# First block's opening on one core: the last modulation chunk in two halves, the first U products ahead of it, the U weights in pieces, the angle tables sooner

## What is computed

```python
mod = jax.nn.silu(c) @ w_ada + b_ada               # 1024 -> 3 * 1024
shift, scale, gate = jnp.split(mod, 3, axis=-1)
h = rms_norm(x, norm_g) * (1 + scale[:, None, :]) + shift[:, None, :]
proj = h @ w_in                                    # q, k, v, gates, u, z_s
...
dt = jnp.exp(log_dt)[:, None]                      # the state space mixer
lam_bar = jnp.exp(lam * dt)                        # complex: powers need sines and cosines
b_bar = ((lam_bar - 1.0) / lam)[..., None] * lax.complex(b_re, b_im)
```

## Time and profile before

| | us |
|---|---|
| three runs: lowest, median, highest | 1003.12, 1003.63, 1003.84 |
| the profiled execution | 1010.04 |
| its span in the trace | 1008.2 |
| busy: PE, DVE, ACT, POOL | 949.0, 579.6, 460.2, 66.5 |

### The profile page before, as it was taken

The page is one execution under the profiler, slowest core; times in us unless marked ns, Lnnn a source line. Parts: engine busy times, 40 slices in busy tenths (PEclk is TensorE's granted clock), DMA queues, the critical chain, the costliest instruction groups (busy, mean ns, idle before and its releaser), DMA issues.

```text
span 1008.2 us, 14233 instructions
## 1 busy us (share of the span) xinstructions
PE 949.0 (94%) x5545; PEld 743.1 (74%) x5545; DVE 579.6 (57%) x1174; ACT 460.2 (46%) x973; POOL 66.5 (7%) x82
## 2 busy tenths in 40 slices
PE   3899999998899999999999998999999999999996
PEld 1479787884456678887678886788888678886784
DVE  2589788863798646153975334636243885334732
ACT  4443542242568534243763436634333772525721
POOL 0100120000170001000010000000000001000000
PEclk9799999999999999999899999999999899999998
DMA  9725245317410023343122323322343222333102
GB/s 361 284 88 126 84 128 170 111 67 192 171 56 2 2 104 121 84 125 104 59 85 84 105 83 106 101 84 84 84 113 95 79 85 64 104 98 111 64 1 83
DMA packets 93588, 104.66 MB, mean 104 GB/s; under 512 B 15777, under 2 KB 63905, under 8 KB 93506
## 3 DMA queue, kind: packets, MB, share of 16 engines
q1 hardware_dynamic: 89410, 87.67, 28.1%
q0 software_dynamic: 3824, 15.73, 4.9%
q10 hardware_dynamic: 288, 0.36, 0.1%
HBM read 98.37 MB, written 4.19 MB: 102 GB/s over the span
## 4 chain that ended last, share of the span: by engine, by line
PE 80%; DVE 7%; ACT 5%; issue 3%; DMA 3%; SPq 1%; DVEq 0%; POOL 0%; POOLq 0%; ACTq 0%; PEldq 0%
PE bank L997 75%; DMA arena<-in_w_ada 2%; DVE ring L1954 2%; PE bank L1305 2%; ACT ring L907 2%; PE bank L1275 1%; DMA ring<-in_w_in 1%; ACT soft L914 1%; PE bank L1443 1%; PE bank L1361 1%; SPq L454 1%; DVE soft L1985 0%; ACT w_hi L857 0%; ACT hT_hi L839 0%; PE bank L1111 0%
## 5 line engine op out<-in xcount | busy, mean ns | idle before, releaser
L1998 DVE TENSOR_TENSOR w_lo<-ring,w_hi 128x1024 fp32r<-128x1024 f32 x80 | 97.8, 1225 | 114.7 <-ACT w_hi L857 111.6
L997 PE MATMUL bank<-w_hi,hT_hi 128*128 128x512 f32 x320 | 125.3, 392 | 1.3 <-issue 1.0
L997 PE MATMUL bank<-hT_hi,w_hi 128*128 128x512 f32 x320 | 125.7, 393 | 0.0
L997 PE MATMUL bank<-w_lo,hT_hi 128*128 128x512 f32 x320 | 124.6, 389 | 0.0
L997 PE MATMUL bank<-hT_lo,w_hi 128*128 128x512 f32 x320 | 124.6, 389 | 0.0
L997 PE MATMUL bank<-hT_hi,w_lo 128*128 128x512 f32 x320 | 124.5, 389 | 0.0
L997 PE MATMUL bank<-w_hi,hT_lo 128*128 128x512 f32 x320 | 124.5, 389 | 0.0
L857 ACT ACTIVATE w_hi<-ring 128x1024 fp32r<-128x1024 f32 x80 | 84.4, 1058 | 11.6 <-PE bank L997 11.4
L997 PEld LDWEIGHTS bank<-w_hi,hT_hi 128*128 128x128 f32 x320 | 60.0, 188 | 14.8 <-issue 2.6
L997 PEld LDWEIGHTS bank<-hT_hi,w_hi 128*128 128x128 f32 x320 | 60.1, 188 | 13.1 <-issue 0.7
L997 PEld LDWEIGHTS bank<-hT_lo,w_hi 128*128 128x128 f32 x320 | 60.1, 188 | 12.6
(11 more groups left out here) (311 smaller groups left out, 1825.4 us busy)
## 6 DMA issues: line engine op xcount, KB each, us to landing
ring<-in_w_in SPq DMA_DIRECT2D x64, 512.0 KB, 4.2
ring<-in_w_ada SPq DMA_DIRECT2D x4, 2048.0 KB, 14.1
ring<-in_w_in SPq DMA_DIRECT2D x4, 2048.0 KB, 9.2
bias_ring<-in_na_bias POOLq DMA_DIRECT2D x8, 1024.0 KB, 5.3
ring<-in_w_out SPq DMA_DIRECT2D x16, 512.0 KB, 3.5
arena<-in_w_ada SPq DMA_DIRECT2D x2, 2048.0 KB, 20.1
ring<-in_w_out SPq DMA_DIRECT2D x2, 2048.0 KB, 9.0
bias_ring<-in_t_bias POOLq DMA_DIRECT2D x8, 448.0 KB, 3.7
```

What stands on the lines that cost most here:

```text
L997: return pe.matmul(out, lhsT, rhs, start=first, stop=last)
L1998: dve.tensor_tensor(w_lo[:, u % 4], raw_w[:, u % 4], w_hi[:, u % 4].bitcast(fp32), SUB).then_inc(S["w_split"], 1)
```

## The change

- SP: chunk 3 is loaded in two halves of four k each (two semaphores); the first 256 columns of U come as two transfers of 128 columns.
- PE: the columns of chunk 2 are made right after its product; chunk 3 is multiplied in two halves, each when it has landed; the unsplit U product starts with k = 0 when `h_raw` is 1, and the columns of chunk 3 are made behind this first k.
- DVE: `h` is scaled in two halves, k = 0 to 3 when the columns of chunk 2 are there. The angle tables are computed ahead of and between the four normalisations of x, and the powers ahead of `h`.
- ACT: the sines are taken behind the transposes, the two small ones ahead of `move_rows(2)`, the two large ones behind it; `move_rows(3)` and `part_hi(1)` stand between the roundings of `h`. Further on, the copies of `bb` and `move_cl(0)` stand earlier.
- POOL: one memset is moved to the start, one behind `cl_ready`.

```diff
-        ada_late_in = [sem(f"ada_late_in_{k}") for k in range(2)]
+        ada_late_in = [sem(f"ada_late_in_{k}") for k in range(3)]
+        u_ahead = [sem(f"u_columns_in_{k}") for k in range(2)]
...
-                  [((KD, 512, 0, 256), wide(win, U0, 256)), ((KD, 512, 256, 512), wide(win, U0 + 256, 256))],
+                  [((KD, 512, 0, 128), wide(win, U0, 128)), ((KD, 512, 128, 256), wide(win, U0 + 128, 128)),
+                   ((KD, 512, 256, 512), wide(win, U0 + 256, 256))],
...
                 if c == SLOTS - 1:
+                    sp.dma_start(ada_late[0], ada[2]).then_inc(ada_late_in[0], 16)
                     for n in range(2):
-                        sp.dma_start(ada_late[n], ada[2 + n]).then_inc(ada_late_in[n], 16)
+                        sp.dma_start(ada_late[1][:, 4 * n:4 * n + 4], ada[3][:, 4 * n:4 * n + 4]).then_inc(ada_late_in[1 + n], 16)
...
             settle(pool.memset(mhalf, -0.5))
+            settle(pool.memset(gate_b[:, :], 0.0))
...
-            pool.wait_ge(S["mod_cols"], 1)
+            pool.wait_ge(S["cl_ready"], 1)
             settle(pool.memset(soft[:, 0:2048], 0.0))
-            settle(pool.memset(gate_b[:, :], 0.0))
...
+            act.wait_ge(S["ang_ready"], 1)
+            act.activation(ang3[:, 0:160], ang[:, 0:160], ACT.Sin).then_inc(S["sin_ready"], 1)
+            act.activation(ang2[:, 0:160], ang2[:, 0:160], ACT.Sin).then_inc(S["sin_ready"], 1)
             move_rows(2)
-            move_rows(3)
+            act.activation(rot_s, ang[:, 160:1184], ACT.Sin).then_inc(S["sin_ready"], 1)
+            act.activation(rot_c, ang2[:, 160:1184], ACT.Sin).then_inc(S["sin_ready"], 1)
...
-            part_hi(1)
             for k in range(KD):
+                if k == 2:
+                    move_rows(3)
+                elif k == 4:
+                    part_hi(1)
                 act.wait_ge(S["h_raw"], k + 1)
                 act.activation(x_hi[:, k, :], hT[:, k, :], ACT.Copy).then_inc(S["h_hi"], 1)
...
-            for n in range(11, 15):
+            part_hi(11)
+            move_cl(0)
+            for n in range(12, 15):
                 part_hi(n)
...
+                elif c == 2:
+                    pe.wait_ge(ada_late_in[0], 16)
+                    times_c(bank[c], ada_late[0]).then_inc(S["ada_done"], 1)
                 else:
-                    pe.wait_ge(ada_late_in[c - 2], 16)
-                    times_c(bank[c], ada_late[c - 2]).then_inc(S["ada_done"], 1)
-                if c:
+                    for n in range(2):
+                        pe.wait_ge(ada_late_in[1 + n], 16)
+                        ins = times_c(bank[c], ada_late[1], range(4 * n, 4 * n + 4))
+                    ins.then_inc(S["ada_done"], 1)
+                if c in (1, 2):
                     mod_columns(c - 1)
-            mod_columns(3).then_inc(S["mod_cols"], 1)
+                if c == 2:
+                    mod_columns(2).then_inc(S["mod_cols"], 1)
...
-            pe.wait_ge(S["u_first"], 16)
+            pe.wait_ge(u_ahead[0], 16)
             for k in range(KD):
                 pe.wait_ge(S["h_raw"], k + 1)
                 ins = mm(bank[0][:, :], p_raw(0)[:, k, :], hT[:, k, :], k == 0, k == KD - 1)
...
+                if k == 0:
+                    mod_columns(3).then_inc(S["mod_cols"], 1)
...
+            turns(ang2, ang)
+            dve.wait_ge(S["x_rstd"], 1)
+            normal(0)
+            normal(1)
+            less_turns(ang, ang2, C1)
+            normal(2)
+            less_turns(ang, ang2, C2)
+            normal(3)
+            less_turns(ang, ang2, C3)
+            within(ang)
+            stt(ang2, ang, -1.0, ang, MUL, MAX)
+            dve.tensor_scalar(ang2, ang2, -1.0, math.pi / 2, MUL, ADD).then_inc(S["ang_ready"], 1)
...
+            modulate(0)
+            dve.wait_ge(S["mod_cols"], 2)
+            modulate(1)
```

More of the change, by code:

```diff
@@ L302, in landed @@
         def landed(c):
-            return 16 * sum(len(chunks[j]) - (j == CH_U) for j in range(c % SLOTS, c + 1, SLOTS))
+            return 16 * sum(len(chunks[j]) - 2 * (j == CH_U) for j in range(c % SLOTS, c + 1, SLOTS))
         def part1(n):
@@ L634, in part_hi @@
                 if n == 1:
-                    act.wait_ge(S["u_first"], 16)
+                    act.wait_ge(u_ahead[1], 16)
                 else:
@@ L707, in move_cl @@
                                    cut(cl_tmp[two * SN:(two + 1) * SN, :], g=GP, m=(LC + 1) * SC), ACT.Copy).then_inc(S["cl_moved"], 1)
+            for i in range(NT):
+                src = proj(PT_KV + i)
+                act.activation(kvs[:, i, :], src[:, 0:256], ACT.Copy).then_inc(S["proj_evac"], 1)
+            part_hi(11)
             move_cl(0)
+            for n in range(12, 15):
+                part_hi(n)
+            for i in range(NT):
+                src = proj(PT_KW + i)
+                act.activation(kvw[:, i, :], src[:, 0:280], ACT.Copy).then_inc(S["proj_evac"], 1)
+            part_hi(15)
             move_cl(1)
@@ L997, in mm, with times_c @@
                 return pe.matmul(out, lhsT, rhs, start=first, stop=last)
-            def times_c(out, w, open_=True):
-                for k in range(KD):
+            def times_c(out, w, ks=range(KD)):
+                for k in ks:
                     r = k % 4 * 32
-                    ins = mm(out[r:r + 32, :], csl_pad[:, k, :], w[:, k, :], open_ and k < 4, k >= 4)
+                    ins = mm(out[r:r + 32, :], csl_pad[:, k, :], w[:, k, :], k < 4, k >= 4)
                 return ins
@@ L1588, in _, with part_lo @@
             dve.tensor_tensor(zr, col("a_re"), s1, MUL).then_inc(S["zr_ready"], 1)
-            dve.wait_ge(S["x_rstd"], 1)
-            for i in range(NT):
-                if i >= 2:
-                    dve.wait_ge(S["xT_done"], 2 * (i - 1))
-                dve.tensor_scalar(xn[:, i % 2, :], x[:, i, :], rstd[:, i:i + 1], None, MUL).then_inc(S["xn_ready"], 1)
+            def part_lo(n):
+                dve.wait_ge(S["p_hi"], n)
+                dve.tensor_tensor(p_lo(n), p_raw(n), p_hi(n).bitcast(fp32), SUB).then_inc(S["p_lo"], 1)
             INV, MAGIC = 1.0 / (2 * math.pi), 1.5 * 2 ** 23
@@ new lines, in _ @@
+            normal(3)
[3 more added lines that the diff above has]
+            dve.tensor_scalar(ang2, ang2, -1.0, math.pi / 2, MUL, ADD).then_inc(S["ang_ready"], 1)
+            dve.wait_ge(S["em_ready"], 1)
+            ts(s2, th, -1.0, 1.0, MUL, ADD)
+            settle(dve.reciprocal(s2, s2))
+            stt(em1, th, 2.0, s2, MUL, MUL)
+            ts(r1, em1, 1.0, None, ADD, ALU.bypass)
+            settle(dve.memset(pw_r[:, 0, :], 1.0))
@@ L1619, in _ @@
+            for j in range(1, LC + 1):
+                tt(pw_r[:, j, :], pw_r[:, j - 1, :], r1, MUL)
+            settle(dve.tensor_copy(r_chunk, pw_r[:, LC, :]))
+            dve.wait_ge(S["sin_ready"], 2)
+            sn, cn = ang3, ang2
+            tt(pw_re, pw_r, cut(cn[:, 0:144], j=LC + 1, g=GP), MUL)
+            tt(pw_im, pw_r, cut(sn[:, 0:144], j=LC + 1, g=GP), MUL)
+            ts(pw_nim, pw_im, -1.0, None, MUL, ALU.bypass)
+            b_ada = col("b_ada")
             dve.wait_ge(S["mod_cols"], 1)
-            b_ada = col("b_ada")
+            dve.wait_ge(S["xT_evac"], 2 * NT)
@@ L1681, in _ @@
             tt(fi, fi, hs, MUL)
-            part_lo(6)
+            part_lo(4)
             dve.wait_ge(S["tables_in"], 32)
@@ L1691, in _ @@
             tt(bi3, bi3, bt3, ADD)
-            part_lo(7)
+            part_lo(5)
             def four(v, n, inner):
```

98 lines of the change are left out of this document (36 added, 62 removed).

## The result

The changed kernel takes **1000.79 us**, the median of 20 runs (998.94 to 1003.38). The kernel before, run beside it, takes 1003.74 (20 runs, 1002.26 to 1011.64). The ratio is 0.9956, with a 95% interval of 0.9939 to 0.9973: a gain of 4.4 us, between 2.7 and 6.1. The ratio goes by all runs, whose means are 1005.29 and 1000.87; the two medians alone lie 2.95 apart, since the runs of before scatter far upwards. The forecast was faster by 7.7 us, 995.9, with a range up to 1000.3. So the sign is right, the gain is too large by some 3 us, and the time lies 0.5 us above the range.

A forecast was written before the change was run, and what follows sets the result against it. PE was taken to bound the kernel, the opening's chain running through w_ada's last chunk. First split product 8.7 us earlier than 49.59, less 1.0 for the clock, gives 7.7; 1003.63 less that is 995.9 us, range 993.9 to 1000.3.

The forecast's parts named there:

- the halves: Opening, w_ada's chunk 3 in two transfers: PE starts the half chunks at 30.4 and 31.5 us, done at 32.45, before 34.45.
- the tables inside DVE's idle time: DVE's opening: small steps and two wide ones, 7.3 us, fit into 7.51 idle; ang_ready's last step ends at 27.0.
- row 2 not late: ACT's small sines end at 28.2 us, just ahead of chunk 2's end at 28.33, so moving row 2 isn't delayed.
- the mark: Start of PE's first split product, 49.59 us before; forecast 40.9 at the high clock, 8.7 us earlier.
- the clock's 1.0: Opening: 1.0 us taken off the gain for PE time at the low clock, within bounds of nothing and 4.4.
- The U piece: First half of U's first transfer: lands at 33.0 us, bounds 31.5 to 34.5, and starts k = 0 of the U product.
- the 34.7 by the fit: U piece's landing by the skill's fit (2.0 us plus bytes over 436 GB/s); would make the sum 1.7 us smaller.
- the term for the opening: First split product 8.7 us earlier than 49.59, less 1.0 for the clock: 7.7 us gain.
- The clock as before: Rival, opening: clock falls at 32.3 us, first split product at 45.3, gain 4.3, time 999.3; chance 0.22.
- The later wait: Rival, behind the opening: ACT's move_cl(0) ahead of Q's first rounding delays PE; 998.9 if 3 us lost; chance 0.10.
- No earlier start: Rival: U piece lands with the old whole, k = 0 at 34.5, 997.4; or 1002 to 1003.6 if h late too; chance 0.07.
- Slower: Rival: DVE's six wide steps blocked, ang_ready 12.1 us late, 11.4 lost, 1007.3; chance 0.03.

The follow-up runs named there:

- the second profile: The changed kernel run and profiled again without any edit: median 999.95 us over 10 runs, ratio 0.9943 to the kernel before.
- wide columns: The changed kernel with column products 64 moving columns wide instead of one: median 1000.45 us, ratio 0.9947 to the kernel before.
- wide columns, before: The kernel before with column products 64 moving columns wide instead of one: median 1003.55 us, ratio 0.9976 to the kernel before.
- the opening's order alone: The kernel before with chunk 3, U's pieces, h and columns reordered; tables and sines unmoved, memsets behind the last columns: 1001.55 us, ratio 0.9951 to before.
- the memsets alone: The kernel before with only POOL's memsets moved, gate_b's to POOL's start and soft's behind the first cl_ready: 1003.61 us, ratio 0.9967 to before.

## Why the gain was forecast too large

**Right, by its steps.** The order in the opening, the halves at 29.80 and 31.56, the tables inside DVE's idle time (`ang_ready` at 26.58 against 27.0), row 2 not late, the mark (41.45 against 40.9 and the clock's 1.0). A microsecond at the mark is one at 91 us behind it. The U piece landed at 33.31, 0.3 us later than forecast; the 34.7 by the fit that the prediction quotes did not come about (the Trainium skill, DMA: Bandwidth & Descriptors, section on the anatomy of one DMA, gives that fit for transfers issued by GpSimd, and these are issued by SP). That the U piece ends the wait for k = 0 holds in the second profile (0.60 us idle); in the first, PE came from the slow second half of chunk 3 without a pause. The clock fell once and for 3.4 us, and cost the mark 0.43 (41.45 against 41.02, or at most 0.9, against the 40.56 with wide columns): the term of 1.0 was large enough. Its remark that no column products alone ran at the high level holds for a long stretch only: those at 28.27 did, for 1.05 us.

**Wrong: one sentence.** "the runs' median is 6.4 lower, and nothing in the opening should differ between them". The whole of 8.7 us was taken from 49.59, a mark that belongs to the profiled execution, and its result was then taken off the median, which belongs to others. So the term for the opening was mis-sized: 8.7 us less 1.0 for the clock, where at an equal clock 3.3 are there, and the rest is what the falls of the clock in that one execution of before had cost. The runs show three things that differ from one execution to the next, two in the opening and one behind it.

The first is the clock: 5.25 of the 8.14 us between the two marks are its price in one execution of before (49.59 against 44.34). What is left, 2.89, is the 3.32 that the change is worth at an equal clock, less 0.43 for the fall after.

The second is when chunk 3 lands. In the 14 profiles, the whole chunk takes 20.6 to 20.9 us from its issue, or 19.3 (wide columns, before); the two halves show a median of 16.0 or 15.3 to 15.4, which puts the second half 1.4 us apart. The row of the issue of both halves in the changed kernel, first and again:

```profile
arena<-in_w_ada SPq DMA_DIRECT2D x2, 1024.0 KB, 16.0
```

```profile
arena<-in_w_ada SPq DMA_DIRECT2D x2, 1024.0 KB, 15.3
```

The packet of instructions is here too. Between 28 and 30 us, in the kernel before, the queues are:

```profile
q1 hardware_dynamic: 482, 0.78, 102.6%
q8 instruction: 1, 0.02, 2.7%
```

It starts at 28.9 to 29.6 us in the eight profiles in which the chunk, or its second half, lands late, and at 30.0 to 30.4 in the six in which it lands early; it takes 0.88 to 1.10 us. The same program shows both (the changed kernel 28.9 and 30.1), so this is a matter of the execution. That the packet is the cause was not tried: no edit here moved it in the opening. What speaks for it is the U piece: it lands at 33.1 to 33.3 behind a late chunk and at 33.2 to 33.5 behind an early one, so the time that an early chunk wins is gone again by then, and behind an early chunk it is the U piece that the packet falls into. The Trainium skill, DMA: Bandwidth & Descriptors, section on queues, rings and completion order, says that a DMA engine takes turns between its queues by whole packets; by that the engine's share of the chunk is held up while the others go on. The traces fit this, with 1.4 us where the packet itself takes about 1; they do not show the engines one by one.

The kernel before bears a late chunk badly: PE then idles 2.2 us, the clock falls, and the marks were 47.4 and 49.6. The one profile with an early chunk (with wide columns) has 44.75. The changed kernel shows 41.02 and 40.97 (the opening's order alone) with an early chunk, 41.45 and 40.56 with a late one, since it waits for the U piece in any case.

The third is the clock behind the mark, and it goes against reading a run's time off its opening. The changed kernel's second profile has the earlier mark (41.02 against 41.45) and the longer time (1003.05 against 1000.55): from the mark to the end it takes 960.2 us, the first 957.4. PE in the changed kernel, 560 to 590 and 870 to 890 us behind the mark (length, busy, clock, DMA share, GB/s), first:

```profile
601.45:631.45 30.00, 26.52 (x264) 1.00 0.37 119
911.45:931.45 20.00, 17.44 (x194) 1.00 0.46 159
```

and again:

```profile
601.02:631.02 30.00, 26.50 (x253) 0.94 0.33 111
911.02:931.02 20.00, 17.71 (x162) 0.83 0.33 114
```

The kernel before shows the same in reverse: its first profile has 0.94 and 0.91 in these two places and takes 958.6 us from the mark, its second 1.00 and 1.00 and 955.9. So of the 4.9 us between the two spans of the kernel before (1008.2 and 1003.3), 2.2 are in the opening and 2.7 behind it. This is what the rival of the last expectation said, low stretches later in the program that the opening doesn't set.

The spread of the runs fits all three: those of before in the three groups of experiments go from 1001.97 to 1010.58, with 28 of 96 below 1004.3 and 45 above 1007, and the changed kernel's 30 from 998.49 to 1003.43. The granted clock of the whole program goes with it: 0.984 to 0.991 in the 28, 0.976 to 0.986 in the 45. Which part of a single run's time comes from the opening its record does not say. The three runs given with the case (1003.12 to 1003.84) were of the lowest part, the profiled one, 1010.04, of the highest. Between the fastest runs the change brings about 3.5 us (1001.97 against 998.49). 1003.63 less 3.3 would have been 1000.3, and 1000.79 was measured; this close an agreement is in part luck, as the means lie 4.4 apart.

**The rivals.** The clock as before (999.3) lies 1.5 us from the measured time, but not by its mechanism: its mark was 45.3, and the changed kernel's profiles have 41.45 and 41.02, with a short fall or none. The later wait: none; the stretch behind the mark is the same. No earlier start: refuted by 33.43. Slower: it did not come, the sine began at 27.34, ahead of the row.

**Open.** Why the memsets alone brought some 3 us. An estimate from rows fits it: the mark of 43.2 for an early chunk and no fall, 0.9 less for the memset, 955.9 from the mark to the end and 1.8 between span and time give 1000.0, and five of its runs lie at 999.45 to 1000.03; no profile shows such a run. Open too: whether wide columns hold the clock; what sets the time of the packet; what decides where behind the mark the clock falls. No version was clearly faster than the changed kernel.

## What to carry to other kernels

If the profiled execution stands far above the runs' median, profile it again, and find out what of a stretch is clock and landing times, and what differs behind it, before taking a difference of marks off the median: price the change at the high clock, and the clock apart, and take its price off only for as many runs as pay it. An idle stretch of PE costs more than its length where the clock falls behind it, and closing it narrowed the spread here too (8.6 us over 96 runs of before, 4.9 over 30 of the changed kernel). Adding instructions is not neutral: it can move a fetch of instructions into a transfer that PE waits for.

## What the runs showed of the hardware that was not expected

- One 16 KB packet of instructions inside a 2 MB transfer goes with a landing over 2 us later (10.4 to 11.1 against 7.8 to 8.3), and with 1.4 us at the end of chunk 3.
- Products with 32 columns of weights take 0.89 us each in the same column position, 0.24 when turned over four.
- Eight column products of 64 moving columns take 2.00 us, of one column 1.95.
- Two executions of the same program differ in where the clock falls 570 and 870 us behind the mark, and by 2.7 to 2.8 us in what they take from there to the end.
- Eight scaled tiles of h beside POOL's memsets take 5.34 us, without them 3.74.
